# Expert weights read in longer runs: gate and up in 512 by 1024 chunks, down in 16 KB runs per partition

## The reference, cut to what matters

```
def expert_choice_ffn(x, router_w, wg, wu, wd):
    ...
    gate, idx = lax.top_k(aff.transpose(0, 2, 1), cap)
    xg = x[bidx, idx]
    hid = jax.nn.silu(jnp.einsum('becd,edf->becf', xg, wg)) * jnp.einsum('becd,edf->becf', xg, wu)
    o = jnp.einsum('becf,efd->becd', hid, wd) * gate[..., None].astype(x.dtype)
    return jnp.zeros_like(x).at[bidx, idx].add(o)
```

## Time and profile before

| | |
|---|---|
| median of three runs | 3578.7 us (3575.94 to 3579.03) |
| span of the profiled execution | 3571.0 us |
| TensorE busy | 3076.2 us, 86% |
| TensorE weight loads, beside it | 1743.0 us, 49% |
| VectorE, ScalarE, GpSimd busy | 951.8, 465.4, 89.2 us |
| moved by DMA | 669.75 MB, 188 GB/s over the span |

### The profile page before, as it was taken

One profiled execution on the slowest core, in us unless ns is written; L12 is line 12 of the kernel. 1 busy time (PEld: TensorE's weight loads), 2 busy tenths in 40 slices (PEclk: granted clock), 3 DMA queues, 4 the chain that ended last, 5 costly groups with the idle time before them and its releaser, 6 DMA issues.

```text
span 3571.0 us, 31927 instructions
## 1 busy us (share of the span) xinstructions
PE 3076.2 (86%) x12698; PEld 1743.0 (49%) x12698; DVE 951.8 (27%) x1836; ACT 465.4 (13%) x874; POOL 89.2 (2%) x156
## 2 busy tenths in 40 slices
PE   3988858787889887988888997899999997899997
PEld 1455423323334443333324575844784575854783
DVE  1156331111122552111101164611101164621101
ACT  1023121111101221111011111110000111110000
POOL 3000000000001000000000000000000000000000
PEclk9986889999999878999999997999999997999999
DMA  9213209999994242999999330044343330043340
GB/s 269 98 49 131 92 1 361 387 387 387 387 387 149 71 171 81 387 387 387 387 387 328 118 118 24 1 167 141 130 142 125 134 118 24 1 162 134 128 143 22
DMA packets 333149, 669.75 MB, mean 188 GB/s; under 512 B 7904, under 2 KB 14312, under 8 KB 333040
## 3 DMA queue, kind: packets, MB, share of 16 engines
q1 hardware_dynamic: 326080, 652.23, 50.7%
q0 software_dynamic: 6960, 15.99, 1.8%
HBM read 667.10 MB, written 2.90 MB: 188 GB/s over the span
## 4 chain that ended last, share of the span: by engine, by line
PE 69%; DMA 16%; DVE 9%; ACT 3%; issue 2%; POOL 0%; another core or an unknown queue 0%; DVEq 0%; ACTq 0%; SPq 0%; POOLq 0%
PE bank L617 40%; DMA ring<-in_exp_w_up_dram 15%; PE bank L628 9%; PE bank L1122 5%; PE bank L938 3%; PE bank L286 2%; PE bank L668 1%; PE bank L901 1%; DMA ring<-in_ada_w_dram 1%; PE bank L962 1%; PE bank L819 1%; PE bank L1097 1%; PE bank L790 1%; PE bank L683 1%; PE bank L1084 1%
## 5 line engine op out<-in xcount | busy, mean ns | idle before, releaser
L617 PE MATMUL bank<-ring,arena 128*128 128x512 f32 (+1 forms) x2176 | 912.0, 581 | 12.3 <-ACT arena L1243 3.3
L628 PE MATMUL bank<-ring,arena 128*64 128x512 f32 (+1 forms) x3072 | 723.2, 622 | 170.5 <-DMA ring<-in_exp_w_up_dram 75.5
L617 PEld LDWEIGHTS bank<-ring,arena 128*128 128x128 f32 x2176 | 413.4, 190 | 503.7 <-issue 497.9
L617 PE MATMUL bank<-arena,ring 128*128 128x256 f32 x2432 | 537.0, 383 | 13.2 <-ACT arena L388 11.1
L628 PEld LDWEIGHTS bank<-ring,arena 128*64 128x64 f32 (+1 forms) x3072 | 204.7, 128 | 663.2 <-issue 451.7
L617 PEld LDWEIGHTS bank<-arena,ring 128*128 128x128 f32 x2432 | 465.2, 192 | 84.8 <-issue 16.1
L286 PE MATMUL bank<-arena 128*128 128x128 f32 (+6 forms) x722 | 136.5, 345 | 162.3 <-DVE arena L1885 28.0
L286 PEld LDWEIGHTS bank<-arena 128*128 128x128 f32 (+6 forms) x722 | 108.5, 182 | 222.3 <-DVE arena L1885 52.1
L1122 PE MATMUL bank<-arena 128*128 128x128 f32 x1376 | 182.7, 294 | 21.5 <-DVE arena L2379 10.5
L1122 PEld LDWEIGHTS bank<-arena 128*128 128x128 f32 x1376 | 173.0, 207 | 33.1 <-DVE arena L2379 13.3
L2062 DVE COPY arena<-bank 128x512 f32<-128x512 f32 (+1 forms) x64 | 44.0, 688 | 522.5 <-PE bank L628 522.5
(11 more groups left out here) (305 smaller groups left out, 1757.3 us busy)
## 6 DMA issues: line engine op xcount, KB each, us to landing
ring<-in_exp_w_gate_dram SPq DMA_DIRECT2D x64, 2048.0 KB, 19.6
ring<-in_exp_w_up_dram SPq DMA_DIRECT2D x64, 2048.0 KB, 19.7
ring<-in_exp_w_down_dram SPq DMA_DIRECT2D x64, 2048.0 KB, 19.7
ring<-in_w_in_dram SPq DMA_DIRECT2D x44, 2048.0 KB, 7.8
ring<-in_ada_w_dram SPq DMA_DIRECT2D x24, 2048.0 KB, 8.1
ring<-in_w_ffn_up_dram SPq DMA_DIRECT2D x20, 2048.0 KB, 7.9
ring<-in_w_out_dram SPq DMA_DIRECT2D x8, 2048.0 KB, 7.8
ring<-in_w_ffn_down_dram SPq DMA_DIRECT2D x8, 2048.0 KB, 7.9
```

Source lines behind the costliest of these rows:

```text
L617: last = mm(o, lhs(k), rhs(k), start=start and k == 0, stop=stop and k == kt - 1)
L628: last = mm(o[g * rows:(g + 1) * rows, :], lhs(k), rhs(k), start=(k < 2), stop=(k >= KT - 2))
```

## The change

Gate and up weights now come in chunks of 512 rows by all 1024 columns (`wide`, [128, 4, 1024]), so that a run is 4 KB: gate rows 0 to 511, gate rows 512 to 1023, up rows 0 to 511, up rows 512 to 1023. The down weights come in two chunks too, but with eight consecutive rows to a partition ("(p k) n"), four of them in each chunk: a run of 16 KB. All other chunks are read as before.

`halved` takes one of two such chunks and feeds two banks, one for each column half; a matrix's first chunk opens the sums in both banks and its second one ends them. With consecutive rows, partition p of the down weights holds hidden features 8p to 8p+7, so the fold must put feature 8n + k at partition n of `HIDT`'s k: its stationary operand now takes every eighth feature of all 1024. For that it needs both column halves of gate and up, and TensorE waits for all four banks' copies ahead of the first fold. The order of units in ScalarE's and VectorE's streams follows (gate, gate, up, up).

```diff
+                if n == D:
+                    eng.dma_start(wide[q % RING], src).then_inc(sem[f"chunk{q % RING}"], 16)
...
-                        for c in range(2):
-                            for w in ("exp_w_gate", "exp_w_up"):
-                                load(A[w][l, g * 4 + e, :, c * CN:(c + 1) * CN])
-                        for c in range(2):
-                            load(A["exp_w_down"][l, g * 4 + e, :, c * CN:(c + 1) * CN])
+                        for w in ("exp_w_gate", "exp_w_up"):
+                            for half in range(2):
+                                rows = A[w][l, g * 4 + e, half * CN:(half + 1) * CN, :]
+                                load(rows.rearrange("(k p) n -> p k n", p=P), n=D)
+                        for half in range(2):
+                            rows = A["exp_w_down"][l, g * 4 + e].rearrange("(p k) n -> p k n", k=KT)
+                            load(rows[:, 4 * half:4 * half + 4, :], n=D)
...
-        def halved(o, rows, lhs, rhs):
-            for k in range(KT):
-                g = k % 2
-                last = mm(o[g * rows:(g + 1) * rows, :], lhs(k), rhs(k), start=(k < 2), stop=(k >= KT - 2))
+        def halved(us, rows, lhs, rhs, half):
+            for c in range(2):
+                for i in range(KT // 2):
+                    k = half * (KT // 2) + i
+                    g = k % 2
+                    last = mm(U(us[c])[g * rows:(g + 1) * rows, :], lhs(k), rhs(i, c), start=(k < 2), stop=(k >= KT - 2))
...
+                if half == 1:
+                    last.then_inc(full[us[c] % BANKS], 1)
...
+                        for n_out in ups:
+                            nc.tensor.wait_ge(free[n_out % BANKS], pe.uses(n_out))
                         for c in range(2):
-                            for n_out in (ups[2 * c], ups[2 * c + 1]):
-                                nc.tensor.wait_ge(free[n_out % BANKS], pe.uses(n_out))
...
-                                              parts[0:2 * M, c, i * P:(i + 1) * P], FOLD[M], start=True, stop=True)
+                                              parts[0:2 * M, :, :].rearrange("p c (n k) -> p k (c n)", k=KT)[:, 4 * c + i, :],
+                                              FOLD[M], start=True, stop=True)
```

More of the change, by code:

```diff
@@ L218, in build @@
         slot = [ring[:, s * KT * CN:(s + 1) * KT * CN].rearrange("p (k n) -> p k n", k=KT) for s in range(RING)]
+        wide = [ring[:, s * KT * CN:(s + 1) * KT * CN].rearrange("p (k n) -> p k n", k=KT // 2) for s in range(RING)]
         U = lambda n: bank[n % BANKS]
@@ L428, in load @@
                     nc.sync.wait_ge(sem["smalls"], sp.due("smalls", 16 * 7))
-                eng.dma_start(slot[q % RING][:, 0:kt, 0:n], src.rearrange("(k p) n -> p k n", p=P)
-                              ).then_inc(sem[f"chunk{q % RING}"], 16)
+                if n == D:
+                    eng.dma_start(wide[q % RING], src).then_inc(sem[f"chunk{q % RING}"], 16)
+                else:
+                    eng.dma_start(slot[q % RING][:, 0:kt, 0:n], src.rearrange("(k p) n -> p k n", p=P)
+                                  ).then_inc(sem[f"chunk{q % RING}"], 16)
             for l in range(DEPTH):
@@ L606, in next_chunk, with next_slot @@
             held[0] = 1
-            return slot[q % RING]
+            return q % RING
+        def next_slot():
+            return slot[next_chunk()]
         def release(ins):
@@ L621, in product @@
             return last
-        def halved(o, rows, lhs, rhs):
-            for k in range(KT):
-                g = k % 2
-                last = mm(o[g * rows:(g + 1) * rows, :], lhs(k), rhs(k), start=(k < 2), stop=(k >= KT - 2))
[L629 to L632, removed]
+        def halved(us, rows, lhs, rhs, half):
[4 more added lines that the diff above has]
+                    last = mm(U(us[c])[g * rows:(g + 1) * rows, :], lhs(k), rhs(i, c), start=(k < 2), stop=(k >= KT - 2))
+                    if pending[0]:
+                        last.then_inc(sem["chunk_used"], 1)
+                        pending[0] = 0
+                if half == 1:
+                    last.then_inc(full[us[c] % BANKS], 1)
         def pe_turn_tiles(src, nt):
@@ L661, in ada @@
                 def ada(j):
-                    w = next_chunk()
+                    w = next_slot()
                     u = pe.unit()
@@ L919, in _ @@
                         ups, halves = [], []
-                        for c in range(2):
[L921 to L930, removed]
-                            for n_out in (ups[2 * c], ups[2 * c + 1]):
-                                nc.tensor.wait_ge(free[n_out % BANKS], pe.uses(n_out))
+                        for w_i in range(2):
+                            us = [pe.unit(), pe.unit()]
+                            for u in us:
+                                nc.tensor.wait_ge(free[u % BANKS], pe.uses(u - BANKS))
+                            for half in range(2):
+                                w = wide[next_chunk()]
+                                halved(us, M, lambda k: XGC[:, e % 2, k, 0:M], lambda i, c: w[:, i, c * CN:(c + 1) * CN], half)
+                            ups += us
+                        for n_out in ups:
+                            nc.tensor.wait_ge(free[n_out % BANKS], pe.uses(n_out))
+                        for c in range(2):
                             u = pe.unit()
@@ L945, in _ @@
                             nc.tensor.wait_ge(free[n_out % BANKS], pe.uses(n_out))
[L946 to L952, removed]
+                        us = [pe.unit(), pe.unit()]
+                        for u in us:
+                            nc.tensor.wait_ge(free[u % BANKS], pe.uses(u - BANKS))
+                        for half in range(2):
+                            w = wide[next_chunk()]
+                            halved(us, M, lambda k: HIDT[:, k, 0:M], lambda i, c: w[:, i, c * CN:(c + 1) * CN], half)
                 nc.tensor.wait_ge(sem["moe_done"], pe.due("moe_done"))
@@ L1423, in _ @@
                             nc.scalar.wait_ge(free[u % BANKS], ac.uses(u))
-                            ac.unit()
+                        ac.unit(2)
                         for c in range(2):
@@ L2057, in _ @@
                     for e in range(4):
+                        dv.unit(2)
                         for c in range(2):
-                            dv.unit()
                             u = dv.unit()
```

## The result

The changed kernel takes 3617.7 us (3612.86 to 3623.67, four runs) against 3577.3 of the kernel before beside it: a ratio of 1.0111, 95% interval 1.0096 to 1.0125, 40 us more. The prediction was 3521, with 3498 to 3568 around it. The first rival, which put the change on the slower side, had said 3622.

A forecast was written before the change was run, and what follows sets the result against it. Transfers were taken to bound both expert stages: 30.7 us saved less 1.9 us of waits gives 28.8 a stage, 57.6 in all, with nothing for strided loads. Forecast 3521 us, range 3498 to 3568.

The forecast's parts named there:

- What bounds the kernel: Both expert stages: DMA engines full at 387 GB/s, 32.5 us an expert; TensorE alone would need 411 or 434 us a stage.
- The DMA's gain: Expert weight chunks: longer runs save 0.30 us per gate or up chunk, 0.41 per down chunk, 30.7 us a stage.
- my 5.12 us: Predicted transfer time of one expert chunk in 4 KB runs, against 5.42 us with 2 KB runs.
- The straight line: Down chunks: packet cost extended from 2 KB and 4 KB to 612 ns for 16 KB, 4.90 us a chunk.
- Rivals 3 and 4: Expert transfers. 3: longer runs save less, 3558 us, 10%. 4: rate unmoved or new reading order costs, 3582 us, 9%.
- The wait before the folds: TensorE waits 0.9 us for VectorE's last copy, uncovered in the last expert; with the ring's start, 1.9 us a stage.
- The strided loads: Fold's weight loads, every eighth feature: nothing to 4.0 us an expert possible, nothing to 2 us taken, covered by the DMA.
- the 223 ns row: Mean time of stationary operands that broadcast one column, against 198 ns for the folds; basis for nothing to 2 us.
- The row that I set aside, 323 ns: Another broadcast stationary operand's mean; gave the upper bound of +125 ns a load, +4.0 us an expert.
- Rival 1: Folds bind in the expert stages: strided loads cost 2.5 times as much, 5.6 us an expert, 3622 us; 9%.
- Rival 2: Folds eat part of the gain: doubled weight loads, 3.75 us an expert, 3563 us; 14%.

The follow-up runs named there:

- e1: The changed kernel with the fold's stationary operand made 128 neighbouring features again, all else kept: 3527.5 us, 0.9856 of before.
- the last version: Changed kernel, each down chunk one feature half in 16 KB runs, PSUM copies permuting by four, contiguous folds needing one half alone: 3507.3 us, 0.9815 of before.
- e6: Changed kernel with half of each expert chunk transferred and folds on neighbouring features, wait for all four copies kept: stages 440.1 and 481.2 us.
- e7: Changed kernel with all runs 4 KB, contiguous folds, no wait for the last copies, half of each expert chunk transferred: stages 420.8 and 437.4 us.
- e5: Changed kernel with only half of each expert chunk transferred, strided loads and wait kept: stages 529.5 and 522.1 us.

## Why the prediction was wrong

**What bounds the kernel: right.** The transfers bound both stages, and with the stride gone (e1) the longer runs gave 52 us, and 69 in the last version.

**The DMA's gain: right, a little too small.** All 4 KB runs give 409 and 410 GB/s in the slices, against 409.6 for my 5.12 us. In the version with 16 KB down runs the window's 415 GB/s make 5.05 us a chunk on the mean; with 5.12 for four of six, a down chunk takes (6 x 5.053 - 4 x 5.12) / 2 = 4.92 us. The same window in layer 1, 1600 to 1700, has 418 GB/s, which makes 4.81. The straight line had given 4.90; I took 5.01. q1's packets fell from 326080 to 203200, by the 122,880 that were named for runs that stay whole. Rivals 3 and 4 fall with that: neither did long runs save less nor did 16 KB out of every 32 KB cost anything.

**The wait before the folds: right where it stands, mis-sized in what follows.** Idle time 1.07 us against my 0.9. But I added the bare 0.9 to TensorE's period. The wait is 63 us of TensorE's own time in both stages (e6 less e7), 1.2 us an expert in layer 0 and 2.7 in layer 1, where the clock falls behind it. TensorE's own length with it was to be 16 x (26.6 + 28.0) = 874 us and was 921. Of the 47 us that were missing, 34 are the wait's; the other 13 are in the undisturbed length, 858 us where one turn of each layer had given 16 x (25.7 + 27.1) = 845. In layer 1 it was 481.2 us, and the first experiment's layer 1 took exactly 481.2 us: there the transfers no longer covered the wait, as I had said they would.

**The strided loads: the step that failed.** I bounded them at 0 to 4.0 us an expert and took 0 to 2, on the ground that the 223 ns row was the nearer one; the sum of the forecast had nothing for them at all, because TensorE's period, at most 30.0 us, was to stay below the transfers' 30.5. They are 4.07 us in layer 0 (7.86 less 3.79), just above the top of the bound: 246 ns a load. The period became 33.2 and 32.6 us, and the transfers no longer covered it. The row that I set aside, 323 ns, is near what the strided loads show, 331 to 335 ns; it is a broadcast and not a stride, so the agreement is taken as chance. The rows could not decide between the two; choosing the low one was a guess and deserved a range that reached the slower side.

**The slow loads were not the whole of it.** With the measured load in place and the rest as predicted, TensorE would need 16 x (26.6 + 28.0 + 2 x 4.07) = 1004 us, 6 less than the stages of before, and the time would have come out near 3573. It needs 1051.6 (e5). The 48 us between are the second thing that was put at too little: the clock, behind the wait, in the slow fold and behind it, and the undisturbed length.

**Rival 1: right in mechanism, its time right by luck.** It asked for loads of 2.5 times, 5.6 us an expert, to reach 3622. The load is 2.1 times as long, and by the rival's own formula one of 250 ns was the point of no change. That its time comes within 5 us of the measured 3617.7 is two errors that cancel, a load too dear and no cost of the clock. Rival 2, at doubled loads, had the right size of the load and said 3563 for the same omission.

**The sum, made again with the measured terms.** Transfers alone were to give stages of 1009.8 - 57.6 = 952.2 us; the last version, where TensorE still waits for chunks, has 946.2. TensorE alone needs 1051.6 (e5). The longer one sets it: 1053.3 measured, 43.5 above before.

## What to carry to other kernels

When a stage bound by transfers is sped up, compute first what its next engine needs in the same stage, with every edit of the change in it, and take that length from a kernel in which the data is there early, not from one or two undisturbed turns. A layout that gives long runs in memory moves a permutation somewhere: put it on an operand of an engine that has time, here the copies out of PSUM, and not on a weight load in a chain of small products. Halving the transfers is a cheap way to ask whether they matter at all. And do not take the price of a pause from its length: the same pause cost 1.2 us an expert in one layer and 2.7 in the other.

## What the runs showed of the hardware

- A float32 weight load of 128 columns in a fold of 32 comes every 117 ns from neighbours at full clock (3.73 to 3.79 us for 32) and every 241 to 246 ns in steps of 16 or 32 bytes (7.70 and 7.86 us). Steps of 8 bytes add little (204 against 202 ns mean), steps of 16 nearly everything (329 against 335).
- The strided pace is the same at a granted clock of 0.90 and of 0.50. The pace of neighbours is not: the same fold took 3.73 us at 1.00 and up to 5.99 us with most of it at 0.50 (e6, layer 1).
- Copies of 128x512 float32 out of PSUM do not slow down when they read in steps of 32 bytes: 692 ns either way by VectorE, 585 and 586 by ScalarE.
- A pause of 1.07 us ahead of each run of small products, 16 times, cost TensorE 19.3 us in layer 0 and 43.8 in layer 1 (e6 less e7). A strided fold, with the pause or without, is followed by 22 to 24 us for 96 products that take 20.8 otherwise in layer 0; in the kernel after the clock stood at 0.50 in the first 1.7 us of them.
- Transfers into SBUF ran at 387 GB/s with 2 KB runs, 410 with 4 KB, and at 415 (layer 0) and 418 (layer 1) on the mean with a third of the bytes in 16 KB runs. The 16 KB runs stay whole: q1 had 122,880 packets fewer.
